# Hybrid decoder step: page buffers, column groups and instruction order changed in the sample attention and the gMLP layer

## The reference

```
layer 0:  u, v, z = split(norm(x) @ w_in)          # each 2048 wide
          v = norm(v) * g_v
          y = u * (tril(w_s) @ v + b_s) * silu(z)  # in chunks of 128 tokens, 8 channel groups
          x = x + y @ w_out
layer 1:  q, k, v, iq, ik, iw, z = split(norm(x) @ w_in)
          scores = sum_h relu(iq_h . ik) * iw_h     # the 256 best keys per row are kept
          att = softmax(q . k_sel / sqrt(128)) @ v_sel
          x = x + (att * silu(z)) @ w_out
```

## Time and profile before

| what | us |
|---|---|
| median of 3 runs (2215.18 to 2216.39) | 2216.26 |
| time of the profiled execution | 2213.05 |
| its span, first to last instruction | 2211.3 |
| TensorE busy in the span | 1999.7 |
| VectorE, ScalarE, GpSimd busy | 999.0, 685.4, 599.5 |

### The profile page before, as it was taken

How to read it: one execution, slowest core, us unless ns; L and a number is a source line. 1 busy time by engine, 2 the same in 40 slices (tenths; PEclk the granted TensorE clock), 3 DMA queues, 4 the chain that set the end, 5 groups by cost and what they waited for, 6 DMA issues and landing times. The chain is left out here.

```text
span 2211.3 us, 33798 instructions
## 1 busy us (share of the span) xinstructions
PE 1999.7 (90%) x12572; PEld 1804.8 (82%) x12572; DVE 999.0 (45%) x1842; ACT 685.4 (31%) x929; POOL 599.5 (27%) x321
## 2 busy tenths in 40 slices
PE   7999998999999999996898888899688988879998
PEld 6999998999999999996763588899455655569898
DVE  3123333111134421424578676789799811231533
ACT  4233332112433332322455222231444532110310
POOL 4333333453333446354110011111100100025221
PEclk8999999999999999997998899999899987789999
DMA  6222222222222233211211203122200014341021
GB/s 167 77 68 76 76 76 76 67 80 83 75 86 85 85 86 86 78 38 49 101 39 26 67 20 88 29 69 79 87 1 1 1 45 154 113 149 47 29 69 41
DMA packets 240516, 152.88 MB, mean 69 GB/s; under 512 B 24946, under 2 KB 235634, under 8 KB 240050
## 3 DMA queue, kind: packets, MB, share of 16 engines
q1 hardware_dynamic: 229314, 140.74, 21.7%
q10 hardware_dynamic: 10192, 9.46, 1.3%
q0 software_dynamic: 928, 1.62, 0.3%
HBM read 135.33 MB, written 16.43 MB: 69 GB/s over the span
## 5 line engine op out<-in xcount | busy, mean ns | idle before, releaser
L392 POOL TENSOR_TENSOR wlo<-wraw,whi 128x1024 fp32r<-128x1024 f32 x177 | 430.5, 2433 | 921.6 <-ACT whi L387 919.9
L404 PE MATMUL PS<-hhi_g,whi 128*128 128x288 f32 (+1 forms) x1536 | 328.3, 295 | 15.3 <-POOL wlo L392 11.1
L404 PE MATMUL PS<-hhi_g,wlo 128*128 128x288 f32 (+1 forms) x1536 | 320.7, 290 | 0.0
L404 PE MATMUL PS<-hlo_g,whi 128*128 128x288 f32 (+1 forms) x1536 | 320.4, 290 | 0.0
L404 PE MATMUL PS<-hhi,whi 128*128 128x364 f32 x1176 | 274.4, 342 | 40.3 <-DVE hlo L1616 12.8
L387 ACT ACTIVATE whi<-wraw 128x1024 fp32r<-128x1024 f32 x177 | 186.6, 1055 | 348.8 <-PE PS L404 310.8
L404 PE MATMUL PS<-hlo,whi 128*128 128x364 f32 x1176 | 265.8, 335 | 0.0
L404 PE MATMUL PS<-hhi,wlo 128*128 128x364 f32 x1176 | 264.6, 334 | 0.0
L404 PEld LDWEIGHTS PS<-hhi_g,whi 128*128 128x128 f32 x1536 | 243.5, 191 | 18.7 <-issue 11.0
L404 PEld LDWEIGHTS PS<-hhi,whi 128*128 128x128 f32 x1176 | 207.0, 194 | 49.6 <-issue 31.7
L404 PEld LDWEIGHTS PS<-hlo_g,whi 128*128 128x128 f32 x1536 | 244.6, 191 | 0.0
(11 more groups left out here) (331 smaller groups left out, 2768.0 us busy)
## 6 DMA issues: line engine op xcount, KB each, us to landing
wraw<-in_w_in_a_dram SPq DMA_DIRECT2D x96, 512.0 KB, 3.9
wraw<-in_w_out_a_dram SPq DMA_DIRECT2D x32, 512.0 KB, 4.1
wraw<-in_w_in_b_dram SPq DMA_DIRECT2D x25, 512.0 KB, 3.8
wraw<-in_w_pe_gate_dram SPq DMA_DIRECT2D x16, 512.0 KB, 4.1
kpg<-in_cache_k_dram SPq DMA_DIRECT2D x64, 128.0 KB, 2.1
vpg<-in_cache_v_dram SPq DMA_DIRECT2D x64, 128.0 KB, 2.0
xs<-xT SPq DMA_DIRECT2D x1, 4368.0 KB, 12.6
xT<-xs SPq DMA_DIRECT2D x1, 4368.0 KB, 13.5
```

The source lines that it names most:

```text
L392: nc.gpsimd.tensor_tensor(wlo[par][:], wraw[par][:], whi[par][:].bitcast(F32), ALU.subtract).then_inc(w_lo, 1)
L404: mm = nc.tensor.matmul(o, w[par][:, k, :], r(k, c0, cn), start=first and i == 0 and n == 0, stop=last and i == KD - 1 and n == 2)
```

## The change

- The second group has 512 columns in one part, so each product is one matmul in one bank; the last four columns of padding are no longer computed. Evictions and norms follow (`np_` is the number of parts).
- ScalarE splits unit 1 of the first group between the sixth and seventh `hhi_g` copy. In the v loops the order of splits and evictions stays what it was, written as eviction of f and split of f+2.
- `kpg` and `vpg` get a third buffer each, where the rotation tables and the even halves `whi`, `wlo` lie; so the split of unit `U_O`+1 waits for the values of sample 5. SP issues keys and values of samples 0 to 2, then keys run two ahead of values.
- TensorE's order in turn b becomes: weights of b (into banks 4 and 5), logits of b+1, keys of b+2, values of b (bank 3).
- The z loads are issued by GpSimd, all eight, when the prompt attention is done. VectorE multiplies the wide part of tiles 0 to 7 in samples 2 to 5, and copies out sample b-1 in the turn of b.
- After the samples the gating of the sample columns runs two tiles ahead of `hlo`.

The diff, cut to its core (what is left out passes `np_` on in the same manner):

```
-GROUPS = [(0, 576, 4, True), (576, 516, 4, False)]
+GROUPS = [(0, 576, 4, True, 2), (576, 512, 4, False, 1)]
 GW = 576
...
         rx = fixed("rx", [P, 9])
+        W0 = at[0] + 2 * KD * P * 4
         wraw = [fixed(f"wraw{s}", [P, KD, P]) for s in range(2)]
...
         qb = pl("qb", [P, DEC_B, NKV, NS])
+        K2 = X0 + sum((w * 4 + 31) // 32 * 32 for w in (NKV * TP, 9 * NKV * DH))
         kout = nc.alloc_sbuf_tensor_at("kout", [P, 9, NKV * DH], F32, offset=H1 + (IH // 2) * TP * 4)
...
         kpg = [pl(f"kpg{q}", [P, NPAGE, NKV * DH]) for q in range(2)]
+        kpg.append(nc.alloc_sbuf_tensor_at("kpg2", [P, NPAGE, NKV * DH], F32, offset=K2))
         rdiag = pl("rdiag", [P, REP, P])
...
         vpg = [pl(f"vpg{q}", [P, NPAGE, NKV * DH]) for q in range(2)]
+        vpg = [[t[:, 0:NPAGE // 2], t[:, NPAGE // 2:]] for t in vpg]
+        vpg.append([nc.alloc_sbuf_tensor_at(f"vpg2{q}", [P, NPAGE // 2, NKV * DH], F32, offset=W0 + q * 2 * KD * P * 4)[:]
+                    for q in range(2)])
         kTb = pl("kTb", [P, NKV, PAST])
...
+            def sample_pages(dst, src, b, done):
+
+                for g in range(NPAGE):
+                    page = sp.value_load(ptab[0:1, b * NPAGE + g:b * NPAGE + g + 1],
+                                         min_val=0, max_val=cache_k.shape[0] - 1)
+                    sp.dma_start(dst(g), src[bass.ds(page, 1), 0].rearrange("a s g d -> s (a g d)")).then_inc(done, 16)
+
+            def key_pages(b):
+                if b >= 3:
+                    sp.wait_ge(sa["kt"], b - 2)
+                sample_pages(lambda g: kpg[b % 3][:, g, :], cache_k, b, kpin[b % 3])
+
+            def value_pages(b):
+                if b >= 3:
+                    sp.wait_ge(sa["pv"], b - 2)
+                sample_pages(lambda g: vpg[b % 3][g // 4][:, g % 4, :], cache_v, b, vpin[b % 3])
+
             sp.wait_ge(w_used, U_O)
-            for b in range(DEC_B):
-                if b == 4:
-                    for q in range(2):
-                        sp.wait_ge(z_st[q], 16 * (KD // 2))
-                    sp.wait_ge(at_["o"], NBLK * NKV)
-                for f in range(2 * b - 8, 2 * b - 6) if b >= 4 else ():
-                    sp.dma_start(zb[f][:], zs[f]).then_inc(z_in[f], 16)
-                for dst, src, used, done in ((kpg, cache_k, sa["kt"], kpin), (vpg, cache_v, sa["pv"], vpin)):
-                    if b >= 2:
-                        sp.wait_ge(used, b - 1)
-                    for g in range(NPAGE):
-                        page = sp.value_load(ptab[0:1, b * NPAGE + g:b * NPAGE + g + 1],
-                                             min_val=0, max_val=cache_k.shape[0] - 1)
-                        sp.dma_start(dst[b % 2][:, g, :],
-                                     src[bass.ds(page, 1), 0].rearrange("a s g d -> s (a g d)")).then_inc(done[b % 2], 16)
+            sp.wait_ge(qq["add"], NH + 1)
+            for b in range(3):
+                key_pages(b)
+                value_pages(b)
+            key_pages(3)
+            key_pages(4)
+            for b in range(5, DEC_B):
+                key_pages(b)
+                value_pages(b - 2)
+            value_pages(DEC_B - 2)
+            value_pages(DEC_B - 1)
             sp.wait_ge(sa["o"], DEC_B)
...
             pool.wait_ge(at_["o"], NBLK * NKV)
+            for q in range(2):
+                pool.wait_ge(z_st[q], 16 * (KD // 2))
+            for f in range(KD):
+                pool.dma_start(zb[f][:], zs[f]).then_inc(z_in[f], 16)
             own.link(nc.gpsimd.memset(acc[:], 0.0))
...
                     norm_hi(act, s, k, *hi)
+                    if k == 5:
+                        split_hi(act, 1, 1, 1)
                     if k in (4, 6):
...
             for g in range(2):
-                c0, n, nch, has_s = GROUPS[g]
-                h = n // 2
+                c0, n, nch, has_s, np_ = GROUPS[g]
+                h = n // np_
                 s = sA[g]
...
                     norm_act(act, nA[g], group_hi(g))
+                else:
+                    split_unit(U_A[g] + 1)
+
                 def v_out_of_psum(f, ff):
...
                     act.wait_ge(s["vtr"], s.at("vtr", f + 1))
-                    nc.scalar.activation(vtmp[ff][:, 0:n].rearrange("p (b n) -> p b n", b=2),
-                                         PS[:, 2 * ff:2 * ff + 2, 0:h], ACT.Copy).then_inc(s["vev"], 1)
+                    nc.scalar.activation(vtmp[ff][:, 0:n].rearrange("p (b n) -> p b n", b=np_),
+                                         PS[:, 2 * ff:2 * ff + np_, 0:h], ACT.Copy).then_inc(s["vev"], 1)
...
                     for ff in range(2):
-                        split_hi(act, (ff + 1) % 2, (U_A[g] + ff + 1) // 2 + i + 1, U_A[g] + 2 * i + ff + 1)
                         v_out_of_psum(2 * i + ff, ff)
-                split_unit(U_A[g] + KA + 1)
+                        split_hi(act, ff, U_A[g] // 2 + i + 2, U_A[g] + 2 * i + ff + 2)
...
                     act.wait_ge(sa["pv"], b)
-                nc.scalar.activation(PsT[:, 0:8, :].rearrange("p k n -> p (k n)"), PS[:, 3, :], ACT.Copy)
-                nc.scalar.activation(PsT[0:NS, 8, :], PS[0:NS, 4, 0:NS], ACT.Copy).then_inc(sa["pt"], 1)
-
-
+                nc.scalar.activation(PsT[:, 0:8, :].rearrange("p k n -> p (k n)"), PS[:, 4, :], ACT.Copy)
+                nc.scalar.activation(PsT[0:NS, 8, :], PS[0:NS, 5, 0:NS], ACT.Copy).then_inc(sa["pt"], 1)
+
+
+            act.wait_ge(sa["pv"], DEC_B - 2)
             split_unit(U_O + 1)
...
+            def sample_out(b):
+                dve.wait_ge(sa["pv"], b + 1)
+                nc.vector.tensor_copy(qT[:, :, b * DEC_T:(b + 1) * DEC_T],
+                                      PS[:, 3, 0:NS].rearrange("p (h t) -> p h t", t=DEC_T)).then_inc(sa["o"], 1)
+
             sample_max(0)
...
                 nc.vector.tensor_scalar(Ps[:], Ps[:], srs[:, b:b + 1], None, ALU.mult).then_inc(sa["nr"], 1)
+                if b:
+                    sample_out(b - 1)
+                for f in range(2 * b - 4, 2 * b - 2) if 2 <= b < 6 else ():
+                    own.link(gate_z(f, slice(NS, TP)))
                 if b + 1 < DEC_B:
                     sample_max(b + 1)
-                dve.wait_ge(sa["pv"], b + 1)
-                nc.vector.tensor_copy(qT[:, :, b * DEC_T:(b + 1) * DEC_T],
-                                      PS[:, 3, 0:NS].rearrange("p (h t) -> p h t", t=DEC_T)).then_inc(sa["o"], 1)
-                for f in range(2 * b - 10, 2 * b - 8) if b >= 5 else ():
-                    own.link(gate_z(f, slice(NS, TP)))
-
-            own.link(gate_z(KD - 2, slice(NS, TP)))
-            own.link(gate_z(KD - 1, slice(NS, TP)))
+            sample_out(DEC_B - 1)
+
+            def gate_sample(f):
+                gate_z(f, slice(0, NS)).then_inc(oy["y"], 1)
+
             dve.wait_ge(sa["o"], DEC_B)
+            gate_sample(0)
+            gate_sample(1)
             for f in range(KD):
-                gate_z(f, slice(0, NS)).then_inc(oy["y"], 1)
                 dve.wait_ge(oy["y"], f + 1)
...
                 nc.vector.tensor_tensor(hlo[:, f, :], qT[:, f, :], hhi[:, f, :].bitcast(F32), ALU.subtract).then_inc(oy["lo"], 1)
+                if f + 2 < KD:
+                    gate_sample(f + 2)
             dve.wait_ge(xs_in, 16)
...
             def k_pages(b):
-                pe.wait_ge(kpin[b % 2], 16 * NPAGE * (b // 2 + 1))
+                pe.wait_ge(kpin[b % 3], 16 * NPAGE * (b // 3 + 1))
                 if b:
                     pe.wait_ge(sa["ke"], b)
+                if b >= 2:
+                    pe.wait_ge(sa["pt"], b - 1)
                 for g in range(NKV):
...
                         tr = nc.tensor.transpose(PS[:, 4 + 2 * g + j // 4, (j % 4) * P:(j % 4 + 1) * P],
-                                                 kpg[b % 2][:, j, g * DH:(g + 1) * DH], ident[:])
+                                                 kpg[b % 3][:, j, g * DH:(g + 1) * DH], ident[:])
                 tr.then_inc(sa["kt"], 1)
...
-            k_pages(0)
-            pe.wait_ge(sa["qc"], 2)
-            sample_logits(0)
-            for b in range(DEC_B):
-                if b + 1 < DEC_B:
-                    k_pages(b + 1)
-                    pe.wait_ge(sa["ke"], b + 2)
+            def sample_turn(b):
                 pe.wait_ge(sa["nr"], b + 1)
+                pe.wait_ge(sa["ke"], min(b + 2, DEC_B))
+                for j in range(NPAGE):
+                    nc.tensor.transpose(PS[:, 4, j * NS:(j + 1) * NS], Ps[:, j * P:(j + 1) * P], ident[0:NS, 0:NS])
+                nc.tensor.transpose(PS[0:NS, 5, 0:NS], Ps[:, PAST:SLS], ident[0:NS, 0:NS]).then_inc(sa["tr"], 1)
+
+            def sample_values(b):
+                pe.wait_ge(sa["pt"], b + 1)
+                pe.wait_ge(vpin[b % 3], 16 * NPAGE * (b // 3 + 1))
                 if b:
                     pe.wait_ge(sa["o"], b)
-                for j in range(NPAGE):
-                    nc.tensor.transpose(PS[:, 3, j * NS:(j + 1) * NS], Ps[:, j * P:(j + 1) * P], ident[0:NS, 0:NS])
```

(39 more changed lines are left out.)

19 lines of the change are left out of this document (9 added, 10 removed).

## The result

The changed kernel takes 2143.13 us (median of 4 runs, 2139.28 to 2145.88), the kernel before on the same chip 2215.72 (2213.23 to 2216.39): ratio 0.9673, 95% interval 0.9656 to 0.969. Forecast were 2149.6, and a range of 2126 to 2174. The same kernel on another chip gave 2141.77, ratio 0.9684 (0.9668 to 0.97).

A forecast was written before the change was run, and what follows sets the result against it. TensorE bounds the kernel, busy 1999.7 of 2211.3 us. Start 6.2, second group 15, sample loop 32.5 and end 13 sum to 66.7 us gained: span 2144.6, or 2149.6 against the median, range 2126 to 2174.

The forecast's parts named there:

- Early split: Start: splitting unit 1 earlier removes TensorE's wait before it and the slow clock after; 6.2 us gained, bounds 3.7 and 6.9.
- Group 2: Second gated group: one 512-column matmul takes 230 ns against 240.2 for the pair; 15 us gained, bounds 9 and 21.
- C: Rival, second group: 512 columns bring nothing, one matmul taking the pair's 240 ns; 2165 us, chance 0.05.
- F: Rival, second group: wide matmuls lose their overhead, 216 ns each, 21 us more gained; 2129 us, chance 0.10.
- E: Rival, second group: the 512-column matmul goes at 428 ns like f32 records, 280 us slower; 2444 us, chance 0.02.
- Loop, work and waits: Sample attention: 12.05 us a sample at full clock, key and page waits gone, first wait stays; 88.5 us from 1800.24.
- Loop, clock: Sample attention: of 29 us going to the half clock, 18 stay lost; loop ends at 1907, 32.5 us earlier.
- B: Rival, sample loop: all 29 us are lost to the half clock as now; 2161 us, chance 0.17.
- A: Rival, sample loop: the clock stays full because no gap is left, 18 us more gained; 2132 us, chance 0.13.
- Pages and z: Sample loop: with three buffers pages land before need, and z loads moved to GpSimd come in time; cost nothing.
- D: Rival, sample loop: pages or z come late, SP's issues hold it to 17.4 us a sample; 2164 us, chance 0.06.
- The end: After the samples: TensorE starts 3.1 us after its last value matmul, an `hlo` every 1.5 us; 13 us gained, bounds 9 and 14.

## Why the prediction was right, point by point

- **Bound.** Right: what was gained is TensorE's idle time, its clock and the dearer matmuls of the second group; its busy time fell by 39.0 us, its idle time by 35.1, and the other engines' busy time moved by under 4 us.
- **Early split.** Direction right, size near the lower end: the forecast was 6.2 with bounds of 3.7 and 6.9, the kernel without it is 3.3 to 5.8 us slower, and 2.3 of the 7.9 us in the table are an earlier start of unit 0. Unit 1 itself ran from 30.3 to 36.64, the 6.4 us of the full clock; in the other traces with the early split it took 6.4 to 7.7, with the late one 8.0. What was not forecast is the wait of 1.89 us inside unit 0. The seventh copy is not to blame, it comes 6.93 us after the start of unit 0 and came 6.81 after it before. VectorE's `hlo_g` behind it is: it runs beside GpSimd's `wlo`, which the early split moved there, and takes 2.08 to 2.19 us for 0.75 in all twelve kernels with the early split (the two with added widths among them), ending 0.61 or 0.62 us after GpSimd each time. The forecast had allowed 0.4 us, for later copies, and nothing for this.
- **Group 2.** Direction right, size too large: the pitch is 233.4 ns and not 230, the pair gains 6.8 and not 10.2 ns, the group 9.7 and not 15 us. The step that failed is the straight line through 258 and 364 columns. 288 (132 ns), 364 (166.1) and 512 (233.4) lie on one line of 0.453 ns a column; by it 258 would take 118.4, and it takes 120.1. A line whose lower point stands 1.7 ns too high is too flat. The overhead of 12.6 and 14.4 ns is 20.1 at 512, so it grows with the columns: the bound of 234 was the right reading. C (nothing gained) and F (216 ns) are out; E too. The formula of the Trainium skill ("TensorE: Matmul & The Clock Gate", "Back-to-back issue gap"), 2.5 ns over N/2.4, is given there for a single matmul by itself. It does not hold for this stream: 6.6 ns over at the faster pitch of 256 columns, 20.1 at 512.
- **Loop, work and waits.** Right. The waits went as forecast, with the first left at 2.95 us. A sample at the full clock takes 11.65 us, not 12.05 (keys run 1.8 behind the logits, and values 4.3), 3 us over the loop.
- **Loop, clock.** The term was mis-sized: the sum's 88.5 us at the full clock become 85.7 with the shorter sample, so 99.0 - 85.7 = 13.3 us stay lost and not 18. The old order shows what the waits did: with a gap of 2.12 us ahead of each turn the clock costs 16.6 us more; without gaps five of seven samples are slow, four of them by 1.6 to 1.7 us each. B (all lost) is out; A (all kept) is out as well, though two samples of seven keep the full clock, the same two in eight traces. That a stretch without a gap can lose it, which the forecast took from the earlier trace rows, was right. The Trainium skill (same page, "Why this matters for your kernels") has the clock kept by matmuls without idle gaps; windows 1803 to 1812 above go against it, as rows 9 did. That the low level would lie on the narrow matmuls was mostly wrong: up to sample 5 they run at 1.00 and the wide ones behind them pay; only the last two samples' values run at half clock.
- **Pages and z.** Right at nothing, and D is out for three buffers. With two it is not: 8.8 us. z on SP or on GpSimd makes no difference.
- **The end.** 13.1 for 13, for the reasons given.
- **The rest.** Nothing was forecast for the stretch behind the third output unit; 3.2 us came. TensorE's work there is the same, and its busy time fell by 3.45 us as the granted clock rose from 0.96 to 0.98, so it is the clock (windows of before and after). With the old order, with two buffers, with the late split or with the gating not spread, what lies behind the last value matmul is again 1.4 to 3.4 us longer than what the edits there explain; why stays open.

```profile
1982.47:2211.30 228.83, 213.42 (x1254) 207.87 (x1254) 70.18 (x71) 40.55 (x48) 71.67 (x36) 0.96 0.16 47
...
1911.58:2137.20 225.62, 209.97 (x1256) 204.71 (x1254) 71.39 (x72) 41.53 (x49) 71.82 (x36) 0.98 0.16 47
```

That the sum came within 7 us is partly luck. A term 5 too large stood beside one 8 too small, and 2.3 us of an earlier start and 3.2 behind the third output unit came unforecast. The mechanism was right for the waits and the end; in the loop the half clock fell on other matmuls than forecast, and at the start an overlap with GpSimd was missed.

Open: what decides whether a sample's logits fall to the half clock. Neither gaps (there were none) nor a long stretch of values (split in halves, it fell six times in one run and twice in another) explains it alone. It is no matter of chance from one execution to the next either, since eight traces of the changed loop have the same five slow samples.

## What to carry to other kernels

Measure the pitch of a matmul at the very width that will be used before padding or merging, and over more than one trace: the pair of 258 columns took 240.2 ns and one matmul of 512 took 233.4, unit after unit, but the pair of 256 took 226.7 or 235.5, on one side of 512 or the other. When an instruction of GpSimd is moved earlier, look at what VectorE does at that time: here one of its subtractions became three times as long. When a turned operand goes through another engine, turn it one sample earlier than needed, since here each wait cost its own length and more than that again in clock. And count issues: a queue that needs longer for a sample's pages than TensorE for the sample lives on its lead, so buffers have to cover the whole loop, not one step.

## What the hardware showed that was not expected

- The pitch of these matmuls has a floor of 111 to 112 ns from 128 to 240 columns. 256 columns have two pitches at one place, 113.3 and 117.8 ns, and keep one of them through a unit: 50 and 13 units in one kernel, 26 and 37 in another with the same second group.
- VectorE's subtraction of two tiles (`hlo_g`, 0.75 us) took 2.08 to 2.19 us beside GpSimd's subtraction of two tiles (`wlo`), and ended 0.61 or 0.62 us after it, in twelve kernels out of twelve.
- Above that, time per column stays at 0.45 to 0.465 ns, 8 to 12% over one column a cycle, from 288 to 512 columns.
- The same instructions in the same order took 95.5 and 101.3 us in two kernels that differ only in work that ends some 900 us earlier.
